# The NSA distance bias built by TensorE and ScalarE instead of loaded, and the keys' decay product moved from VectorE to GpSimd

## The reference, cut to what matters

```python
def hgrn2_scan(q, k, v, logf):      # mixer B; k is 1 - f, forward and backward
    ...
    b = jnp.cumsum(l_, axis=2)
    dec = exp(b_t - b_s) where s <= t, else 0
    attn = einsum('bhtk,bhsk,bhtsk->bhts', q_, k_, dec)
    o_intra = einsum('bhts,bhsv->bhtv', attn, v_)
    ...
def rel_bucket(dist):
    n = jnp.maximum(dist, 0)
    large = 16 + (log(max(n, 1) / 16) / log(128 / 16) * 16).astype(int32)
    return jnp.where(n < 16, n, jnp.minimum(large, 31))
# NSA: score(t, s) * SCALE + rel_table[rel_bucket(t - s), head], masked where s > t
```

## Time and profile before

| what | value |
|---|---|
| median of three runs | 2651.54 us |
| profiled execution | 2650.95 us, span 2649.0 us |
| TensorE, matmuls busy | 2504.9 us, 95% |
| VectorE busy | 1768.1 us, 67% |
| ScalarE busy | 853.6 us, 32% |
| GpSimd busy | 332.2 us, 13% |
| mean granted TensorE clock | 0.974 |

### The profile page before, as it was taken

How to read it: one execution, slowest core, us unless ns; L and a number is a source line. 1 busy time by engine, 2 the same in 40 slices (tenths; PEclk the granted TensorE clock), 3 DMA queues, 4 the chain that set the end, 5 groups by cost and what they waited for, 6 DMA issues and landing times.

```text
span 2649.0 us, 45224 instructions
## 1 busy us (share of the span) xinstructions
PE 2504.9 (95%) x16992; PEld 2340.2 (88%) x16992; DVE 1768.1 (67%) x3570; ACT 853.6 (32%) x2161; POOL 332.2 (13%) x368
## 2 busy tenths in 40 slices
PE   5968999988999999999999999989999999999998
PEld 4857888877888878899999999988888999999998
DVE  6885664585465563499888885433737998878744
ACT  2532210254211022212565551022432136655300
POOL 0020100002001001001111112100320021111221
PEclk8989999999999999999999999998899999999999
DMA  8425887520687862379999999963014899999998
GB/s 328 134 81 216 307 303 287 196 81 21 223 302 265 320 254 95 104 240 400 357 401 389 405 404 416 414 247 127 17 64 152 307 364 389 408 384 407 406 415 344
DMA packets 171353, 726.99 MB, mean 274 GB/s; under 512 B 19024, under 2 KB 19536, under 8 KB 146256
## 3 DMA queue, kind: packets, MB, share of 16 engines
q1 hardware_dynamic: 143568, 523.92, 53.3%
q0 software_dynamic: 27648, 201.34, 18.8%
HBM read 724.13 MB, written 1.05 MB: 274 GB/s over the span
## 4 chain that ended last, share of the span: by engine, by line
PE 84%; DVE 7%; DMA 4%; ACT 3%; issue 2%; SPq 0%; DVEq 0%; ACTq 0%; POOLq 0%
PE banks L706 38%; PE banks L952 21%; PE lev L994 19%; PE lev L706 3%; DMA ring<-in_peer_v 2%; PE lev L935 1%; PE banks L935 1%; PE lev L1019 1%; DMA extra<-in_ada 1%; DVE nmax L1659 1%; ACT arena L1216 1%; DVE arena L1657 1%; DVE rstd L1615 1%; DVE arena L1739 0%; DVE arena L1598 0%
## 5 line engine op out<-in xcount | busy, mean ns | idle before, releaser
L706 PE MATMUL banks<-hT,ring 128*128 128x256 f32 x2832 | 633.1, 387 | 42.1 <-ACT hT L1169 41.2
L706 PEld LDWEIGHTS banks<-hT,ring 128*128 128x128 f32 x2832 | 549.1, 194 | 124.7 <-issue 45.7
L994 PE MATMUL lev<-arena,ring 128*128 x4096 | 579.0, 301 | 3.4 <-DMA ring<-in_peer_v 3.3
L952 PE MATMUL banks<-hT,ring 128*128 128x160 f32 x4096 | 579.6, 302 | 0.0
L994 PEld LDWEIGHTS lev<-arena,ring 128*128 128x128 f32 x4096 | 559.2, 190 | 5.6 <-issue 5.5
L952 PEld LDWEIGHTS banks<-hT,ring 128*128 128x128 f32 x4096 | 561.7, 191 | 0.9 <-issue 0.3
L1569 POOL DMA_INDIRECT arena<-in_peer_rows,keysb x192 | 214.9, 1119 | 1142.4 <-DVE consts L1916 628.8
L706 PE MATMUL banks<-arena,ring 128*128 128x256 f32 (+1 forms) x1344 | 288.5, 379 | 3.4 <-DMA ring<-in_stream_first 3.4
L706 PEld LDWEIGHTS banks<-arena,ring 128*128 128x128 f32 x1344 | 255.0, 200 | 35.4 <-issue 3.7
L1960 DVE SCALAR_TENSOR_TENSOR extra<-consts,chT 128x192 bf16<-128x192 f32 x640 | 223.5, 408 | 7.9 <-ACT arena L1260 7.8
L706 PE MATMUL lev<-arena 128*128 128x128 f32 (+1 forms) x976 | 159.2, 315 | 29.3 <-DVE arena L1774 21.2
(11 more groups left out here) (271 smaller groups left out, 2291.5 us busy)
## 6 DMA issues: line engine op xcount, KB each, us to landing
ring<-in_peer_u SPq DMA_DIRECT2D x256, 512.0 KB
ring<-in_peer_v SPq DMA_DIRECT2D x256, 512.0 KB
ring<-in_stream_first SPq DMA_DIRECT2D x192, 512.0 KB
arena<-in_ada SPq DMA_DIRECT2D x104, 512.0 KB, 5.3
extra<-in_ada SPq DMA_DIRECT2D x88, 512.0 KB, 4.9
ring<-in_stream_nsa SPq DMA_DIRECT2D x45, 512.0 KB
ring<-in_stream_fox SPq DMA_DIRECT2D x41, 512.0 KB
arena<-in_peer_rows,keysb POOLq DMA_INDIRECT x192
```

The source lines that it names most:

```text
L706: ins = nc.tensor.matmul(o, lhsT, rhs, start=start, stop=stop, **kw)
L952: ins = nc.tensor.matmul(banks[k // 2 % 4][:, (k % 2) * ND:(k % 2 + 1) * ND], ring[:, u % RING, c], hT[:, c, NS:T], start=c == 0, stop=c = ...
L994: ins = nc.tensor.matmul(lev[c // 4][:, (c % 4) * T + NS:(c % 4 + 1) * T], ring[:, u % RING, c], a[:, bass.ds(g, 1), k], start=False, stop ...
```

## The change

Two edits, independent of each other.

The bias table. The host now sends a 128 x 560 array in place of the 128 x 4096 one: a strip of 512 columns that holds, three times below each other and shifted by one column each, the one-hot code of the bucket for every distance (33 rows each, the last for masked positions), and the 33 x 16 table three times on a block diagonal (48 columns). Where the program had only the transfer, TensorE now makes, right after `norm_stat(6)`, one matmul for every three key positions: the stationary operand is a 128-column window of the strip, the moving one the 48 columns of the table. There are 86 of them, ten to a bank, in nine new jobs `relb` that stand in the job list between `norm 6` and `nin 0`. ScalarE, after `norm(6)`, copies each bank into the bias table (eight of 128x480, one of 128x256), then goes on to `cbias`. VectorE's wait for the transfer goes, TensorE waits for it instead.

```diff
+REL_SHIFTS = P // (REL_BUCKETS + 1)      # 3
+REL_W = REL_SHIFTS * NSA_H               # 48
+REL_COLS = 10 * REL_SHIFTS               # 30
+REL_JOBS = -(-256 // REL_COLS)           # 9
...
+        relc = place(2 * T + REL_W)
         bias = place(NSA_H, T)
...
         plan(("norm", 6), 1)
+        plan(("relb",), REL_JOBS)
...
                     sp.wait_ge(sem("sums_y"), 1)
-                    sp.dma_start(bias.rearrange("p h k -> p (h k)"), io["rel"]).then_inc(sem("rel_in"), 16)
+                    sp.dma_start(relc, io["rel"]).then_inc(sem("rel_in"), 16)
...
             norm_stat(6)
-
+            pe.wait_ge(sem("rel_in"), 16)
+            relt = relc[:, 2 * T:2 * T + REL_W]
+            for k in range(0, T, REL_SHIFTS):
+                i = k % REL_COLS
+                if i == 0:
+                    b = open_job("relb", k // REL_COLS)
+                s = P - k + T - 1
+                end = i == REL_COLS - REL_SHIFTS or k + REL_SHIFTS >= T
+                mm_(b[:, i * NSA_H:i * NSA_H + REL_W], relc[:, s:s + P], relt,
+                    filled("relb", k // REL_COLS)[0] if end else None)
...
             norm(6)
-            wait(sem("rel_in"), 16)
+            for k in range(REL_JOBS):
+                n = min(REL_COLS, T - k * REL_COLS)
+                wait(*filled("relb", k))
+                A(bias[:, :, REL_COLS * k:REL_COLS * k + n], bank_of("relb", k)[:, 0:n * NSA_H]
+                  .rearrange("p (k h) -> p h k", h=NSA_H), ACT.Copy).then_inc(freed("relb", k)[0], 1)
+
+            wait(*freed("relb", REL_JOBS - 1))
             wait(sem("nsa_zero"), 1)
```

```diff
             for l in range(DEPTH):
+                for k in range(8):
+                    pool.wait_ge(sem("decays"), (l * 8 + k + 1) * 4)
+                    pool.wait_ge(sem("keys_ready"), l + 1)
+                    G.tensor_tensor(ek[:, k % 2], ek[:, k % 2], fk, ALU.mult).then_inc(sem("keys_decayed"), 1)
                 attention(("att", l), units_of(l), l * NATT)
...
                         wait(sem("decays"), (l * 8 + k + 1) * 4)
-                        V.tensor_tensor(ek[:, k % 2], ek[:, k % 2], fk, ALU.mult).then_inc(sem("keys_decayed"), 1)
                         seq(V.tensor_tensor(eq[:, k % 2], eq[:, k % 2], qB, ALU.mult), "queries_decayed")
```

More of the change, by code:

```diff
@@ L146, in mixer_constants, with bucket_strip @@
     return np.concatenate([al.reshape(P, -1)] + [a.astype(np.float32) for a in lm] + [causal], 1).astype(np.float32)
-def distance_rows():
-    n = P + np.arange(P)[:, None] - np.arange(T)[None]
+def bucket_strip():
+    n = np.arange(2 * T) - (T - 1)
     nf = np.maximum(n, 1).astype(np.float32)
@@ L154, in distance_rows @@
     b = np.where(n < 16, np.maximum(n, 0), np.minimum(large, REL_BUCKETS - 1))
-    return np.where(n >= 0, b, REL_BUCKETS)
+    one = np.zeros((REL_BUCKETS + 1, 2 * T), np.float32)
+    for k in range(REL_BUCKETS):
+        one[k] = (b == k) & (n >= 0)
+    one[REL_BUCKETS] = n < 0
+    out = np.zeros((P, 2 * T), np.float32)
+    for r in range(REL_SHIFTS):
+        out[r * (REL_BUCKETS + 1):(r + 1) * (REL_BUCKETS + 1), r:] = one[:, :2 * T - r]
+    return out
 def tile_unit(w):
@@ L215, in lay_out @@
     order = [(2 * gg + hh) * 4 + j for gg in range(2) for j in range(4) for hh in range(2)]
-    table = np.concatenate([g["rel_table_2"][:, order], np.full((1, NSA_H), NEG, f32)], 0)
-    out["rel"] = np.ascontiguousarray(table[distance_rows()].transpose(0, 2, 1)).reshape(P, NSA_H * T)
+    rel = np.zeros((P, REL_W), f32)
+    for r in range(REL_SHIFTS):
+        at, cols = r * (REL_BUCKETS + 1), slice(r * NSA_H, (r + 1) * NSA_H)
+        rel[at:at + REL_BUCKETS, cols] = g["rel_table_2"][:, order]
+        rel[at + REL_BUCKETS, cols] = NEG
+    out["rel"] = np.concatenate([bucket_strip(), rel], 1)
     out["c_rows"] = np.ascontiguousarray(np.stack([np.broadcast_to(g["c"][0], (P, D)), np.broadcast_to(g["c_2"][0], (P, D))], 1))
```

## The result

The changed kernel takes 2693.7 us (median of four runs, 2689.23 to 2694.78) beside 2651.24 us of the kernel before on the same chip: ratio 1.0146, interval 1.0132 to 1.0161. The two medians are 42 us apart. The ratios with their intervals are the record's and are not the quotient of the two medians; this one stands for + 35 to + 43 us. I had forecast 2681 us, + 30 us, with a range up to 2688.

The account below looks back on a forecast made before the run. TensorE was taken to bound the kernel (busy 95% of the span). On 2650.95 us, 25.6 (bias step) + 1.0 (slower projection) + 3 (keys' product) = + 29.6 us, stated as 2681 us; range 2677 to 2685, widened to 2669 to 2688.

Parts of the forecast that it names:

- the keys' product, + 3 us in the sum: Attention levels: moving 16 VectorE products to GpSimd costs + 1.5 us per block, as the two engines exclude each other.
- The two levels that I did price, 6 and 7: End of each block's levels: GpSimd's product holds VectorE 1.7 us where 1.14 is spared, + 0.6 us twice.
- The upper bound of that term: Keys' product in the levels: at most 4 x (2.9 - 1.14) = + 7.0 us.
- The bias: NSA stretch: 172 matmul records take 31.1 us before the first projection, 25.6 us beyond the gap; 26.6 us in all.
- gap of 5.47: TensorE's wait for hT between statistics and first projection, 5.47 us, claimed to hide that much of the new bias step.
- The + 1.0 us for a slower first projection: Projection behind the new bias step: at least 2.1 us more at half clock, + 1.0 us.
- Rival (b): New bias step: the clock stays full throughout, 18.1 us less the gap; kernel at 2667 us; chance 6%.
- rival (d): New bias step: costs only its columns, 6.9 us, weight loads hide; with VectorE relieved, 2648 us; chance 3%.
- The mechanism of the exclusion: Levels: GpSimd's product and VectorE instructions with two SBUF inputs block each other; hold 1.7 us for 1024 elements.
- (a): Levels: GpSimd's product fits beside VectorE's one-input or PSUM work, tails up to 2.3 us earlier per block; 2674 us; 15%.
- (c): Levels: GpSimd's hold near 2.9 us, or TensorE's new level 6 gaps cost clock; 2685 to 2687 us; 10%.

Follow-up runs that it names:

- run 3: Only the keys' product moved to GpSimd, bias still loaded, against the kernel before: 2664.17 us, ratio 1.0035.
- Run 4: Keys' product on GpSimd at levels 0 to 5 only, levels 6 and 7 on VectorE, against the kernel before: 2661.95 us, ratio 1.0031.
- run 2: Only the bias edit, keys' product back on VectorE, against the kernel before: 2681.57 us, ratio 1.0108.
- run 5: Kernel before with all keys' products on VectorE, plus an unneeded 128x768 GpSimd product at each of the 16 places: 2676.34 us, ratio 1.0082.
- run 8: Kernel before with only the keys' products of levels 2 and 4 on GpSimd, released under VectorE's reciprocals: 2655.07 us, ratio 1.0002.
- run 9: Bias edit alone in bfloat16, with ScalarE's first six bank copies ahead of hT, against the kernel before: 2653.06 us, ratio 0.9994.
- run 7: Bias edit alone with its matmuls in bfloat16 (table loses its low bits), against the kernel before: 2659.27 us, ratio 1.0025.

## Why the prediction was wrong

**The step that failed: the keys' product, + 3 us in the sum.** Alone it measures + 9.5 us (run 3). The main error was where the cost arises; the size of one hold and the number of meetings were off as well. First the hold: I scaled 0.43 us of a 256-element product to 1.7 us for 1024; the traces show 2.03 to 2.20 us. The Trainium skill (GPSIMD Engine Reference, § 3.1), whose ratio I did not follow, was nearer: 2.4 us by it as an estimate for the instruction, and 2.35 us were measured. Second, and most of it, where it costs. I had written that at levels 1 to 5 what is late "by a microsecond I count at nothing", and that VectorE is the bound "from level 6 on". The trace before has VectorE at work with 0.29 us of idle time from 93.20 us to the rotary step, so it was the bound from level 2 on. Run 4 shows the price: each of the six products of levels 0 to 5 held a difference, an `eq` or a step of a norm, VectorE entered the rotary step 4.4 us late per block, and TensorE waited anew at level 3 (1.68 us) and level 5 (1.51 us). The two levels that I did price, 6 and 7, measure + 1.1 us together in the first block where I had + 1.2: that part was right. A waits view with three entries said that TensorE had cover at the other levels; it did not say how little. Before, `eq` of level 3 was ready at 108.64 us and TensorE started that level at 108.82 us. Third, the number of meetings: I priced six (levels 0, 6 and 7 of each block); in both blocks all eight took place.

**The upper bound of that term** was 4 x (2.9 - 1.14) = + 7.0 us and is exceeded for the same reason: it counted the tail's meetings alone. Two smaller things helped to put the time outside the range of 2669 to 2688 us, and they are chance: I started from 2651 us, where the kernel before has 2654.0 over all its runs, and the first four runs of the changed kernel lie on the high side of its scatter. With the measured terms the sum is 2654.0 + 26.9 + 9.5 = 2690.4 us, beside 2690.3 over all runs.

**The bias: right, its last microsecond by luck.** Clock at 1.00 for 5 us and then 0.50 as said; gap of 5.47 covered; no wait for the transfer or for ScalarE's copies; + 26.6 us forecast, + 26.9 measured (run 2). Within the sum two errors cancel. The step takes 32.3 us from start to start in run 2, 1.2 more than the 31.1 forecast. The + 1.0 us for a slower first projection is not there: the three projections up to `compress` take 22.49 us in run 2 as before. In the changed kernel they take 23.04 us, and `compress` behind them 22.60 in place of 23.11. Rival (b), the full clock, and rival (d), columns alone, did not come. One small slip changed nothing: a projection takes 7 us there and not 6.

**The mechanism of the exclusion: right**, in both directions, shown by run 5. The rivals (a) and (c): nothing came forward in the levels, so (a) falls. (c) at 2685 to 2687 us was the nearest by its number, and I gave it 10%; its reasons did not come. The hold was 2.03 us and not near 2.9, and TensorE's level 6 ran at half clock (0.50) before as well (3.76 us, 3.61 us in the changed kernel). A dearer exclusion is what came, but at levels that neither (c) nor the forecast had priced.

**The scatter: not seen.** The kernel before spans 2645.5 to 2663.2 us over 79 runs, and I took the median of three runs, two of which agreed, as its place. In 75 of the runs the granted clock is listed: its mean goes from 0.969 to 0.976, correlates with the time at - 0.89, and 0.001 of it goes with 2.4 us. Two medians of four runs can therefore differ by several microseconds without any cause in the kernel.

## What to carry to other kernels

Moving a product from VectorE to GpSimd can pay only if what VectorE does meanwhile does not take both inputs from SBUF. Beside the one-input reciprocals it cost nothing (run 8); beside instructions with two it held VectorE 2.03 of its 2.35 us where 1.14 us were spared. Count every meeting, also where TensorE did not wait before: look for idle time in VectorE's own stream ahead of the wait. Float32 matmuls with 48 columns went at the pace of their two weight loads, and the granted clock fell to 0.50 during them; where TensorE is the bound, a table whose load is hidden is cheaper loaded than computed, unless the computing fits a gap (run 9). When a step becomes faster, look at which buffers it will now fill (run 7): the wait that appears is one of order, and can be removed by order (run 9).

## What was not expected of the hardware

- GpSimd's 128x1024 product takes 2.35 us and holds VectorE 2.03 us of it (86%); the 128x256 product took 0.73 us and held 0.40 (55%). A shorter instruction is held less: a step of the rotary part 1.30 us at level 6.
- A record with its weight load costs nearly the same with 48 columns at the lower clock (210 ns) and with 256 columns at the full one (217 ns): 32 us against 37.3 us for the step, whose first 5 us ran at the full clock with 48 columns too.
- bfloat16 records with the same 128x128 weight take 29 ns at a clock of 1.00 (40 in 1.16 us) and 49 ns at 0.50 (46 in 2.25 us), and 39 ns at 1.00 for the whole step in run 9 (86 in 3.36 us), where float32 ones take 106 ns at 1.00 and 210 ns at 0.50, and one is needed in place of two.
